# The mask of the diagonal block in three attention phases: from TensorE products to in-place additions on VectorE

## What is computed

```python
for blk in range(S // 128):
    lo, hi = blk * 128, (blk + 1) * 128
    s = einsum('bhmqd,bhmkd->bhmqk', q[lo:hi], k[:hi]) * scale   # m: two maps (differential), one (mla)
    p = softmax(where(mask, s, -inf))                            # mask differs from all-true
    a = p[map 0] - lam * p[map 1]                                # only in the last 128 columns
    out = a @ v[:hi]                                             # mla: a = p
```

## Time and profile before

| | us |
|---|---|
| median of three runs (4027.2 to 4030.54) | 4028.1 |
| the profiled execution, its own time | 4022.91 |
| span of the profiled execution | 4021.1 |
| TensorE matmul busy in the span | 3400.3 |
| VectorE busy | 2374.9 |
| ScalarE busy | 1875.8 |
| mean granted clock of TensorE | 0.919 |
| differential attention, about 288 to 566 | 278 |
| first mla, about 2834 to 3057 | 223 |
| second mla, about 3580 to 3804 | 224 |

### The profile page before, as it was taken

The page is one execution under the profiler, slowest core; times in us unless marked ns, Lnnn a source line. Parts: engine busy times, 40 slices in busy tenths (PEclk is TensorE's granted clock), DMA queues, the critical chain, the costliest instruction groups (busy, mean ns, idle before and its releaser), DMA issues. The chain is left out here.

```text
span 4021.1 us, 52306 instructions
## 1 busy us (share of the span) xinstructions
PE 3400.3 (85%) x17620; PEld 2687.7 (67%) x17620; DVE 2374.9 (59%) x3722; ACT 1875.8 (47%) x3128; POOL 308.8 (8%) x374
## 2 busy tenths in 40 slices
PE   8988979599999448786999992699895979989778
PEld 7876658488888324575888882578674757877656
DVE  3226666799988637548999885551234645313276
ACT  3115641378888310115788882331345623224474
POOL 0000001000000110000000002000001300000032
PEclk9999989699999769887999996899997989999879
DMA  6322234499999665436999996442223234322232
GB/s 236 106 69 62 64 99 165 161 399 398 399 398 398 240 242 184 160 129 229 399 398 399 399 398 216 168 157 81 61 49 119 98 134 157 115 59 49 74 130 78
DMA packets 411311, 791.67 MB, mean 197 GB/s; under 512 B 99942, under 2 KB 154758, under 8 KB 408968
## 3 DMA queue, kind: packets, MB, share of 16 engines
q1 hardware_dynamic: 388108, 705.61, 48.6%
q0 software_dynamic: 13824, 50.34, 3.6%
q10 hardware_dynamic: 9216, 33.56, 2.1%
HBM read 653.45 MB, written 135.95 MB: 196 GB/s over the span
## 5 line engine op out<-in xcount | busy, mean ns | idle before, releaser
L312 DVE TENSOR_TENSOR experts_down_lo<-weights_down,experts_down_hi 128x1024 fp32r<-128x1024 f32 x256 | 301.1, 1222 | 56.5 <-ACT experts_down_hi L308 54.2
L312 DVE TENSOR_TENSOR experts_gate_lo<-weights_gate,experts_gate_hi 128x1024 fp32r<-128x1024 f32 x256 | 298.8, 1222 | 52.1 <-ACT experts_gate_hi L308 51.4
L308 ACT CAST experts_gate_hi<-weights_gate 128x1024 fp32r<-128x1024 f32 x256 | 254.2, 1056 | 106.5 <-PEq L126 67.8
L312 DVE TENSOR_TENSOR experts_up_lo<-weights_up,experts_up_hi 128x1024 fp32r<-128x1024 f32 x256 | 296.3, 1221 | 1.2 <-ACT experts_up_hi L308 0.5
L359 PE MATMUL project_acc<-project_wh,project_hh 128*128 128x512 f32 (+2 forms) x768 | 286.1, 373 | 0.0
L360 PE MATMUL project_acc<-project_wl,project_hh 128*128 128x512 f32 (+2 forms) x768 | 282.3, 368 | 0.0
L361 PE MATMUL project_acc<-project_wh,project_hl 128*128 128x512 f32 (+2 forms) x768 | 282.3, 368 | 0.0
L308 ACT CAST experts_down_hi<-weights_down 128x1024 fp32r<-128x1024 f32 x256 | 255.8, 1052 | 24.9 <-DMA weights_down<-in_moe_w_down_dram 24.7
L308 ACT CAST experts_up_hi<-weights_up 128x1024 fp32r<-128x1024 f32 x256 | 253.9, 1056 | 7.8 <-DMA weights_up<-in_moe_w_up_dram 6.2
L2248 ACT COPY project_row<-project_acc 128x512 f32<-128x512 f32 (+2 forms) x96 | 51.8, 540 | 380.0 <-PE project_acc L361 380.0
L359 PE MATMUL experts_yp<-experts_down_hi,experts_hTh 128*128 128x512 f32 x512 | 210.6, 411 | 13.1 <-DVE experts_hTl L312 13.1
(11 more groups left out here) (427 smaller groups left out, 8045.8 us busy)
## 6 DMA issues: line engine op xcount, KB each, us to landing
weights_gate<-in_moe_w_gate_dram SPq DMA_DIRECT2D x256, 512.0 KB, 12.9
weights_up<-in_moe_w_up_dram SPq DMA_DIRECT2D x256, 512.0 KB, 12.2
weights_down<-in_moe_w_down_dram SPq DMA_DIRECT2D x256, 512.0 KB, 11.4
scratch_y<-experts_y ACTq DMA_DIRECT2D x64, 512.0 KB, 6.3
pool_ada<-in_ada_w_dram SPq DMA_DIRECT2D x16, 1536.0 KB, 7.7
project_raw<-in_w_in_dram SPq DMA_DIRECT2D x8, 2048.0 KB, 9.8
scratch_proj<-project_row SPq DMA_DIRECT2D x64, 256.0 KB, 2.0
qkv_raw<-in_attn_w_qkv_dram SPq DMA_DIRECT2D x48, 256.0 KB, 3.4
```

Source lines behind the costliest of these rows:

```text
L308: return act.copy(hi, src)
L312: return dve.tensor_tensor(lo, src, hi.bitcast(F32), ALU.subtract)
```

## The change

The 256 products of identity and mask are gone (two parts of 96 pairs; the differential phase has two maps), with the two ScalarE copies that prepared them in each phase and the semaphore `masks_ready`. Instead VectorE adds the mask to the last 128 columns in place in PSUM, right before the maxima of the same part: 192 additions, in mla of 128x128, in the differential phase of 128x256, since one instruction takes both maps. Behind each addition stands a wait of VectorE on its own semaphore.

```diff
-        identr, maskr = ph.sb("identr", [P, P], F32R), ph.sb("maskr", [P, P], F32R)
...
                             for mp in range(maps):
                                 rows_ = slice(mp * dk, (mp + 1) * dk)
-                                nc.tensor.matmul(scores_of(n, part, mp)[:, c:c + w], qT[rows_, h % 2, i * P:(i + 1) * P],
-                                                 kT[rows_, h % 2, c:c + w], start=True, stop=(c + w < cols))
-                        for mp in range(maps):
-                            last = nc.tensor.matmul(scores_of(n, part, mp)[:, cols - P:cols], identr[:, :], maskr[:, :],
-                                                    start=False, stop=True)
+                                last = nc.tensor.matmul(scores_of(n, part, mp)[:, c:c + w], qT[rows_, h % 2, i * P:(i + 1) * P],
+                                                        kT[rows_, h % 2, c:c + w], start=True, stop=True)
                         last.then_inc(s_ready, 1)
...
-                pe.wait_ge(masks_ready, 2)
...
-                act.copy(identr[:, :], K["ident"]).then_inc(masks_ready, 1)
-                act.copy(maskr[:, :], mask).then_inc(masks_ready, 1)
...
+                def masked(n, part):
+                    cols = (tiles_of(n)[part] + 1) * P
+                    if diff:
+                        both = s_ps[:, 0:4 * HALF] if part == 0 else s_ps[:, 4 * HALF:]
+                        at = both.rearrange("p (m c) -> p m c", m=2)[:, :, cols - P:cols]
+                        ch(dve.tensor_tensor(at, at, mask.unsqueeze(1).to_broadcast([P, 2, P]), ALU.add))
+                    else:
+                        at = scores_of(n, part, 0)[:, cols - P:cols]
+                        ch(dve.tensor_tensor(at, at, mask, ALU.add))
+                    ch.wait()
...
                     dve.wait_ge(s_ready, 2 * n + 1)
+                    masked(n, 0)
                     for mp in range(maps):
                         dve.tensor_reduce(bias[:, n % 2, mp:mp + 1], scores_of(n, 0, mp), AX.X, ALU.max,
                                           negate=True).then_inc(bias_ready, 1)
                     dve.wait_ge(s_ready, 2 * n + 2)
+                    masked(n, 1)
```

More of the change, by code:

```diff
@@ L628, in phase_attention @@
         (k_in, q_in, k_ready, k_copied, q_ready, q_copied, t_ready, t_copied, s_ready, bias_ready, exp_done, a_ready,
-         o_ready, o_done, own, masks_ready) = (ph.sem(n) for n in (
+         o_ready, o_done, own) = (ph.sem(n) for n in (
             "k_in", "q_in", "k_ready", "k_copied", "q_ready", "q_copied", "t_ready", "t_copied", "s_ready", "bias_ready",
-            "exp_done", "a_ready", "o_ready", "o_done", "own", "masks_ready"))
+            "exp_done", "a_ready", "o_ready", "o_done", "own"))
         v_in, stored = ([ph.sem(f"{n}{b}") for b in range(2)] for n in ("v_in", "stored"))
```

## The result

| | before | after |
|---|---|---|
| median of 18 runs each, us | 4027.44 | 4036.25 |
| ratio, 95% interval | | 1.0023 (1.0016 to 1.0029) |
| span of the profiled execution | 4021.1 | 4038.3 |
| differential attention, first load to next phase's first load | 277.3 | 267.0 |
| first mla, first load to next phase's VectorE work | 222.8 | 231.3 |

The kernel became slower by 0.23%, 8.8 us. The three phases make -10.3 + 8.5 + 9.1 = +7.3 us of it. The two profiled executions lie 17.2 us apart; the 9.9 us that are missing stand in phases that the change does not touch, above all between the differential attention and the first mla (2268.4 us before, 2278.2 after). Over the thirteen profiled executions of this study that stretch lasted 2268.4 to 2278.6 us, so I read nothing of the change from one such difference.

What follows compares the result with a forecast made beforehand. TensorE sets the pace, but late hand-overs from VectorE and ScalarE count. Mla +12.8, differential phase -10.5 and uncovered first scores +0.6 sum to +2.9 us, added to the 4028.1 median: 4031 us, range 4016 to 4048.

Steps and rivals of the forecast that it cites:

- the rival with the dearer addition: Third rival: additions in PSUM cost more than 0.33 us in mla, about 4044 at 0.40, 4057 at 0.46; chance 0.34.
- The hand-overs: In mla TensorE's L746 waits for VectorE's output scaling L900; in the differential phase a late maximum holds ScalarE's exponential.
- The price of an addition: On VectorE, 0.29 + 0.04 = 0.33 us in mla and 0.42 + 0.04 = 0.46 in the differential phase.
- mla: the mechanism: VectorE's additions delay L900 and so L746, each shift passing whole into the next pair: 6.4 us a phase, +12.8 for two.
- The 1024-column pair: In mla, L900 and with it L746 come 0.56 us later, as VectorE already sets the pace there.
- The other three pairs: In mla, L746 comes later by 0.11 us at 896 columns, 0.15 at 768 and 0.05 at 640.
- The products: In mla TensorE saves 0.10 us for each of two products, 0.20 a pair, lost in the wait for VectorE.
- The bounds: Lower and upper price of an addition: some 14 us under before, 4014, and +29, 4057.
- The differential phase: Dropped products win 0.65 us in two pairs and 0.16 at 640 columns; 1024 loses 0.17; -10.5 us in all.
- The clock should stay at 1.00 in both.: TensorE's granted clock stays at 1.00 in the profiles, one of the signs named for the profile after.

Runs made afterwards that it cites:

- scaling moved: Changed kernel with the output scaling in mla put between the wide and narrow maxima instead of behind them; 4022.80 us, 0.9984 to before.
- wide part alone: Changed kernel, but in mla VectorE masks only the wide part and the narrow part keeps its product; 4021.11 us, 0.9988 to before.
- doubled additions: Changed kernel with every addition in mla done twice, the second waiting for the first; 4107.72 us, 1.0191 to before.
- no mask: Kernel before with neither products nor additions in mla, so its diagonal blocks stay unmasked; 4019.72 us, 0.9978 to before.
- mixed: Changed kernel, but wide parts of 1024 columns and all narrow parts of mla keep their products; 4007.76 us, 0.9947 to before.
- products of zeros: Changed kernel with TensorE keeping its 256 products, of identity and a tile of zeros; 4052.17 us, 1.0065 to before.

## Why the prediction was right, and which step failed

Forecast 4031 us, 2.9 slower; measured 4036.25, 8.8 slower and inside the range of 4016 to 4048. The forecast's likeliest outcome was no change beyond 0.2% (chance 0.49). The measured 0.23% lies just over that line, where the rival with the dearer addition stood (0.34), but its mechanism did not occur. The hand-overs came out as described. That the sum came near was partly luck: its terms were 7 us too high, and the clock, which it left out, put 11 on top.

**The price of an addition: right.** 0.295 us for 128 columns and 0.424 for 256, and 0.03 to 0.04 for the wait, against 0.29, 0.42 and 0.04. Writing PSUM in place cost nothing more, so the third rival's mechanism is out. The Trainium skill's statement that a semaphore between two VectorE operations costs nothing (VectorE: DVE Perf Modes, "The DRAIN you can't avoid"), measured there on a chain of copies, does not hold here: 0.08 us before the end without a late wait, 0.03 to 0.04 after it with one. The same section also says that a next operation that is not held starts earlier, and with that the 0.08 agrees.

**mla: the mechanism right, two terms off.** The head grew by 0.63 and not by 0.87. The 1024-column pair paid 0.45 instead of 0.56: I had L900 follow L874 at 0.05 us, as before. After the change L906 starts 0.08 before the end of L880, without a late wait, so the 0.13 us had been a wait of L900 for TensorE, too short to be listed as idle. The other three pairs paid 0.03, 0.09 and 0.06, 0.18 together instead of 0.31; I have not taken these apart. The products cost TensorE 0.16 a pair and not 0.20, which by itself works the other way. Times 16 heads the forecast was some 4 us too high. (The bounds counted both additions in the 640-column pair and the sum only one; this makes the range about 2 us wider at either end and changes nothing else.) The kernels with the scaling moved, with the wide part alone and with doubled additions show the hand-over itself.

**The differential phase: right in sum, for two reasons that cancelled.** The phase took 10.3 us less, forecast 10.5 - 0.2. A free head won 1.51 us instead of 1.29. From one wide maximum to the next, beginning with the 1024-column pair, its distances were 7.32, 8.23, 8.14 and 8.06 before and are 7.52, 7.45, 7.39 and 7.89 now, so +0.20, -0.78, -0.75 and -0.17, where the forecast had +0.17, -0.65, -0.65 and -0.16. The surplus stands in the two pairs of 896 and 768 columns. The 896-column pair went from 408.00 to 416.23 before (the pair of the earlier trace rows) and from 403.88 to 411.30 after, 0.81 us shorter instead of 0.65; from the start of its scores to the transposes it was 2.98 and is 2.14, 0.84 less, where two pairs of products account for 0.65. The other 0.19 is in the score passes themselves. Before, the eight wide passes start here, the first pair of products comes 1.70 us later, and the four narrow passes take 0.63 from 410.07 to the second pair at 410.70:

```profile
408.00 1.77 PE L725 MATMUL diff_s<-diff_kT,diff_qT 64*128 64x512 f32 x8
```

That is 2.33 us for twelve passes; after the change the same twelve take 2.14, with nothing of 128 rows between them. This fits the Trainium skill (TensorEngine Tiling (Array Packing), "Key Properties"): changing the tiling mode drains TensorE, and after the change wide and narrow scores follow in one mode. No experiment here takes the change of mode away and leaves the products, so the 0.19 is measured and its cause is only argued. Two stretches of half clock, 1.7 us each, took back the 3.4 us that the phase would have won beyond the forecast.

**The step that failed: "The clock should stay at 1.00 in both."** I had left the clock out of the sum, the range and the rivals. The changed kernel loses 2 x 1.7 us in the differential phase and 2.95 + 3 x 1.65 = 7.9 in mla (heads of 31.94, 29.42 and 28.1 against 30.24 and 26.47), 11.3 in all; run once more, 9.9. Without them the three phases would stand at about -13.7 + 9.7 = -4 us instead of +7.3, where the forecast had +2.9. So by these sums, of one recorded execution each, the clock and not the additions decides the sign.

What lets it fall is settled only in part. In mla the stretches come only in kernels with an addition in the wide part of the 1024-column pair (six kernels, the changed one twice), never without it (six kernels, among them one with as few instructions of TensorE a head as the changed kernel). The traces show what these kernels have in common. The rows are the stretch from the 1024-column pair's wide maximum to the next one in an undisturbed head of mla: before, no mask, mixed; then wide parts alone, scaling moved, products of zeros, changed.

```profile
2897.84:2904.21 6.37, 5.65 (x38) 4.47 (x38) 1.78 (x4) 3.37 (x8) 0.00 (x0) 1.00 0.00 0
2900.50:2906.75 6.25, 5.53 (x36) 4.34 (x36) 1.71 (x4) 3.48 (x8) 0.00 (x0) 1.00 0.00 0
2887.50:2894.14 6.64, 5.92 (x40) 4.69 (x40) 2.09 (x6) 3.37 (x8) 0.00 (x0) 1.00 0.00 0
2893.30:2899.89 6.59, 5.64 (x37) 4.38 (x36) 2.00 (x6) 3.47 (x8) 0.00 (x0) 1.00 0.00 0
3003.20:3009.78 6.58, 5.65 (x36) 4.23 (x35) 2.29 (x7) 3.48 (x8) 0.00 (x0) 1.00 0.00 1
2990.60:2997.48 6.88, 5.65 (x38) 4.42 (x37) 2.29 (x6) 3.47 (x8) 0.00 (x0) 1.00 0.00 0
2899.50:2906.32 6.82, 5.45 (x36) 4.17 (x35) 2.30 (x7) 3.47 (x8) 0.00 (x0) 1.00 0.00 0
```

TensorE is idle 0.72 us of it in the first three, which have no stretch in mla, and 0.95, 0.93, 1.23 and 1.37 in the last four, which have one, eight, three and four. All seven wait 0.59 for the keys; for VectorE's scaling the first three wait 0.07 or less, the last four 0.30, 0.18, 0.58 and 0.71. The differential phase goes the same way. From the wide maximum of its 1024-column pair to the next TensorE is idle 1.03 us before and in the mixed kernel, 1.25 with products of zeros, all without a stretch, and 1.79 in the changed kernel, which has two; there the second wait is that for ScalarE (0.10, 0.10, 0.32 and 0.86). So every kernel with stretches has TensorE idle longer in that pair, by a second wait close to the one for the keys. An addition there does not suffice, and neither does a little more idle time: the kernel with products of zeros has both in the differential phase, and no stretch. How often the clock falls does not follow the idle time: moving the scaling cut it and the stretches rose from four to eight. A kernel that adds there while TensorE has other work in the gap was not tried, so whether the wait or something else of the addition counts in mla stays open.

Also open: whether some of the differential phase's gain is given back before the first mla. That stretch took 2268.4 to 2274.2 us in the four executions whose differential phase lasts about its old length, and 2272.0 to 2278.6 in the nine others; the two ranges overlap, and one execution each does not tell.

## What to carry to other kernels

Moving a small step to an idle engine is free only where that engine is not the last at the next hand-over: read, pair by pair, who starts right at whose end, and move the step only in the pairs that have the slack. Here the mask of the wide part, moved by itself, was worth -0.11 to -0.12 us in three pairs of an mla head and +0.22 in the fourth, and moving it only in the right parts made 20 us of gain out of 9 of loss. Look too at what a new wait does to TensorE's granted clock: in the changed kernel the falls cost 11.3 us, more than the 9.7 of the hand-over. A gap of a few hundredths between two instructions of one engine can already be a wait, where their neighbours overlap.

## What the runs showed of the hardware that I had not expected

The granted clock of TensorE can fall from 1.00 to 0.50 in the midst of a phase in which it is busy 23.2 of 26.5 us a head, with no single wait over 0.72 us ahead of it, for 3.4 to 6.8 us at a time, at 1.6 to 3 us each; the kernel before is busy 23.55 of 25.84 and did not show it in its recorded execution. A mean clock of the whole execution hardly tells: 0.919 before, 0.916 after. Between 64-row score passes in the differential phase a pair of 128-row products cost TensorE, beside its own time, 0.19 us more in the passes around it (read in one pair of column blocks, 896 with 256). VectorE's addition in place in PSUM took the same 0.29 us as one that writes SBUF.
